# Prompt attention, first three query tiles: two pairs in flight on one PSUM bank per group, with constant products beside them

## What is computed

```python
s = jnp.einsum('bqgrd,bngd->bqgrn', qg, kc.astype(f32))
p = masked_softmax(s, (cmp_end[None, :] <= tq)[None, :, None, None, :])
o_cmp = jnp.einsum('bqgrn,bngd->bqgrd', p, vc.astype(f32))
...
o = g[..., 0:1] * o_cmp + g[..., 1:2] * o_slc + g[..., 2:3] * o_win
```

## Time and profile before

| | us |
|---|---|
| median of 3 runs | 3641.18 (3640.17 to 3641.56) |
| profiled execution, its own time | 3649.14 |
| span of its trace | 3647.7 |
| TensorE busy | 3419.4 |
| VectorE busy | 1495.8 |
| ScalarE busy | 868.0 |
| GpSimd busy | 642.9 |
| mean granted TensorE clock | 0.971 of full |
| prompt attention starts and ends in the span | about 939.5 and 1280 |

### The profile page before, as it was taken

The page is one execution under the profiler, slowest core; times in us unless marked ns, Lnnn a source line. Parts: engine busy times, 40 slices in busy tenths (PEclk is TensorE's granted clock), DMA queues, the critical chain, the costliest instruction groups (busy, mean ns, idle before and its releaser), DMA issues. The chain is left out here.

```text
span 3647.7 us, 64454 instructions
## 1 busy us (share of the span) xinstructions
PE 3419.4 (94%) x26955; PEld 2950.4 (81%) x26955; DVE 1495.8 (41%) x2726; ACT 868.0 (24%) x1649; POOL 642.9 (18%) x433
## 2 busy tenths in 40 slices
PE   8899998998878869999999998999999999999999
PEld 5666666554446649999999998888879999999999
DVE  4565666422466662323232323534424332322322
ACT  2333222011256622211011112433323211111110
POOL 0000000204000004222222223221113321222221
PEclk9999999999699989999999999999999999999999
DMA  2000000303200041211111102111113111111111
GB/s 105 22 20 8 26 10 12 135 24 82 77 1 2 1 167 41 76 58 52 45 41 46 48 33 102 35 54 66 38 76 118 53 50 36 51 35 45 47 40 66
DMA packets 77731, 186.33 MB, mean 51 GB/s; under 512 B 28412, under 2 KB 42556, under 8 KB 75468
## 3 DMA queue, kind: packets, MB, share of 16 engines
q1 hardware_dynamic: 60892, 141.85, 11.3%
q0 software_dynamic: 12272, 40.38, 3.4%
q10 hardware_dynamic: 4352, 1.05, 0.1%
HBM read 159.45 MB, written 27.92 MB: 51 GB/s over the span
## 5 line engine op out<-in xcount | busy, mean ns | idle before, releaser
L196 PE MATMUL ps<-ff_x,ff_wh 128*128 128x384 f32 (+1 forms) x3960 | 774.8, 328 | 0.0
L196 PEld LDWEIGHTS ps<-ff_x,ff_wh 128*128 128x128 f32 x3960 | 668.6, 188 | 0.8
L196 PE MATMUL ps<-ff_x,ff_wl 128*128 128x384 f32 (+1 forms) x2112 | 465.4, 328 | 0.0
L196 PEld LDWEIGHTS ps<-ff_x,ff_wl 128*128 128x128 f32 x2112 | 360.6, 188 | 0.0
L559 DVE TENSOR_TENSOR resid<-resid,ps 128x384 f32 (+1 forms) x240 | 113.3, 528 | 390.1 <-PE ps L196 390.1
L196 PE MATMUL ps<-ff_hh,ff_dh 128*128 128x384 f32 (+1 forms) x1056 | 233.8, 329 | 9.2 <-DVE ff_hl L551 4.8
L196 PE MATMUL ps<-ff_hh,ff_dl 128*128 128x384 f32 (+1 forms) x1056 | 233.4, 329 | 0.0
L196 PE MATMUL ps<-ff_hl,ff_dh 128*128 128x384 f32 (+1 forms) x1056 | 233.2, 329 | 0.0
L546 DVE TENSOR_TENSOR ff_prod<-ff_silu,ps 128x384 f32<-128x384 f32 x132 | 62.3, 528 | 349.5 <-PE ps L196 349.5
L279 POOL TENSOR_TENSOR ff_wl<-ff_w,ff_wh 128x1024 fp32r<-128x1024 f32 x44 | 111.9, 2543 | 500.4 <-ACT ff_wh L422 500.4
L196 PEld LDWEIGHTS ps<-ff_hh,ff_dh 128*128 128x128 f32 x1056 | 180.3, 188 | 11.0 <-DVE ff_hl L551 5.9
(11 more groups left out here) (609 smaller groups left out, 6192.2 us busy)
## 6 DMA issues: line engine op xcount, KB each, us to landing
ff_w<-in_wg SPq DMA_DIRECT2D x44, 512.0 KB, 3.2
ff_w<-in_wu SPq DMA_DIRECT2D x44, 512.0 KB, 3.3
ff_wd<-in_wd POOLq DMA_DIRECT2D x48, 256.0 KB, 3.0
ff_wd<-in_wd POOLq DMA_DIRECT2D x32, 320.0 KB, 3.3
rw_w<-in_w_rwkv SPq DMA_DIRECT2D x14, 512.0 KB, 3.4
ns_past<-in_cache_slc SPq DMA_DIRECT2D x48, 128.0 KB, 2.1
np_w<-in_w_nsa SPq DMA_DIRECT2D x8, 652.0 KB, 7.8
resid<-in_x SPq DMA_DIRECT2D x1, 4352.0 KB, 14.9
```

The costliest lines, as they stand in the source:

```text
L196: mm = pe.matmul(g.ps[:, bank + c, 0:n], w[:, k, :], x[:, o:o + n], start=(first and i == 0), stop=(last and i == 2))
```

## The change

For the first 24 pairs (`short = 24`, query tiles 0 to 2, where the scores and the 63 compressed columns fit in one bank):

- the scores of a pair take one bank per group, 0 or 1 for group 0 and 2 or 3 for group 1, by the parity of the pair; the compressed part stands at column 448 of the bank;
- the scores of y wait for the exponentials of y-2 in place of y-1;
- TensorE issues scores 0 and 1, then 16 products of 384 columns in BF16 from constants (identity and masks), and then for each pair its transposes, the scores of y+2, the values of y-1;
- for pairs below 16, each step of transposes has one such product ahead of it, into the bank that the step writes;
- ScalarE does the exponentials of pairs 0 and 1 first; then for each pair all moves of y and then the exponentials of y+2;
- VectorE does the maxima of pairs 0 and 1 and the scaling of pair 0, and then for each pair the scaling of y+1 ahead of the maxima of y+2.

From pair 24 on all is as before.

```diff
+    short = 24
+    def score_banks(y, gr):
+        b = 2 * gr + (y % 2 if y < short else 0)
+        return g.ps[:, b:b + 1, :] if y < short else g.ps[:, b:b + 2, :]
+    def compressed_of(y, gr):
+        at = 448 if y < short else 768
...
-                if y >= 1:
+                if y >= short:
                     pe.wait_ge(expd, 2 * y)
+                elif y >= 2:
+                    pe.wait_ge(expd, 2 * y - 2)
...
                 if x >= 2:
                     pe.wait_ge(moved, x - 1)
+                if y < 16:
+                    spare_products(pe, g.ps[:, 4 + x % 2, 0:3 * P], ident, every_mask, 1)
...
             scores(0)
+            scores(1)
+            spare_products(pe, g.ps[:, 4, 0:3 * P], ident, every_mask, 16)
             for y in range(len(pairs)):
-                if y + 1 < len(pairs):
+                if short <= y + 1 < len(pairs):
                     scores(y + 1)
                 xs = of_pair[y]
                 for x in xs[0:2]:
                     turn(x)
+                if y + 2 < short:
+                    scores(y + 2)
                 if y >= 1:
                     values(y - 1)
...
             act.wait_ge(blank, 2)
-            exponent(0, 0)
-            exponent(0, 1)
+            for y in range(2):
+                for gr in range(2):
+                    exponent(y, gr)
             for y in range(len(pairs)):
                 xs = of_pair[y]
+                if y < short:
+                    for x in xs:
+                        move(x)
+                    for gr in range(2):
+                        if y + 2 < short:
+                            exponent(y + 2, gr)
+                        if y == short - 1:
+                            exponent(short, gr)
+                    continue
...
-            maxima(0, 0)
-            maxima(0, 1)
+            for y in range(2):
+                for gr in range(2):
+                    maxima(y, gr)
+            for gr in range(2):
+                weights(0, gr)
             for y in range(len(pairs)):
-                for gr in range(2):
-                    weights(y, gr)
+                for z in ([y + 1] if y + 1 < short else [] if y < short else [y]):
+                    for gr in range(2):
+                        weights(z, gr)
                 if y % 8 == 1 and y > 8:
                     store(y // 8 - 1)
-                if y + 1 < len(pairs):
+                for z in ([y + 2] if y + 2 < short else [y + 1] if short <= y + 1 < len(pairs) else []):
                     for gr in range(2):
-                        maxima(y + 1, gr)
+                        maxima(z, gr)
```

More of the change, by code:

```diff
@@ L980, in size, with scores_of @@
         return len(keys(t, part)) + part
+    short = 24
+    def score_banks(y, gr):
+        b = 2 * gr + (y % 2 if y < short else 0)
+        return g.ps[:, b:b + 1, :] if y < short else g.ps[:, b:b + 2, :]
+    def scores_of(y, gr, n):
+        return score_banks(y, gr).rearrange("p a n -> p (a n)")[:, 0:n]
+    def compressed_of(y, gr):
+        at = 448 if y < short else 768
+        return score_banks(y, gr).rearrange("p a n -> p (a n)")[:, at:at + NCMP]
     steps = [(y, a, min(4, 2 * size(y) - a)) for y in range(len(pairs)) for a in range(0, 2 * size(y), 4)]
@@ L999, in nsa_prompt @@
         ident, causal, window = (masks[:, x, :] for x in range(3))
+        every_mask = masks[:, :, :].rearrange("p a n -> p (a n)")
         @block.sync
@@ L1041, in scores @@
                     for gr in range(2):
-                        mm = pe.matmul(g.ps[:, 2 * gr + a // 512, 0:m], q[gr], g.kT[f[gr], 1 + part, lo + a:lo + a + m], start=True, stop=not inside)
+                        mm = pe.matmul(scores_of(y, gr, n)[:, a:a + m], q[gr], g.kT[f[gr], 1 + part, lo + a:lo + a + m], start=True, stop=not inside)
                 for a in range(0, n, 512):
@@ L1046, in scores @@
                         for gr in range(2):
-                            mm = pe.matmul(g.ps[:, 2 * gr + a // 512, j * P - a:j * P - a + P], ident, over[j], start=False, stop=(j == inside[-1]))
+                            mm = pe.matmul(scores_of(y, gr, n)[:, j * P:j * P + P], ident, over[j], start=False, stop=(j == inside[-1]))
                 if part == 1:
-                    out = [g.ps[:, 2 * gr + 1, 256:256 + NCMP] for gr in range(2)]
+                    out = [compressed_of(y, gr) for gr in range(2)]
                     for gr in range(2):
@@ L1104, in exponent @@
                 n = len(keys(t, part)) * P
-                b = 2 * gr
                 act.wait_ge(maxed, i + 1)
@@ L1109, in exponent @@
                 x = prob[part][:, gr, :]
-                s = g.ps[:, b:b + 2, :].rearrange("p a n -> p (a n)")[:, 0:n]
-                a = act.activation(x[:, 0:n], s, ACT.Exp, bias=top[:, i % 4, 0:1], accum_out=total[:, i % 4, 0:1])
+                a = act.activation(x[:, 0:n], scores_of(y, gr, n), ACT.Exp, bias=top[:, i % 4, 0:1], accum_out=total[:, i % 4, 0:1])
                 if part == 1:
-                    a = act.activation(x[:, 640:640 + NCMP], g.ps[:, b + 1, 256:256 + NCMP], ACT.Exp, bias=top[:, i % 4, 1:2],
+                    a = act.activation(x[:, 640:640 + NCMP], compressed_of(y, gr), ACT.Exp, bias=top[:, i % 4, 1:2],
                                        accum_out=total[:, i % 4, 1:2])
@@ L1148, in maxima @@
                     dve.wait_ge(expd, i - 3)
-                s = g.ps[:, b:b + 2, :].rearrange("p a n -> p (a n)")[:, 0:n]
-                m = dve.tensor_reduce(top[:, i % 4, 0:1], s, AX, ALU.max, negate=True)
+                m = dve.tensor_reduce(top[:, i % 4, 0:1], scores_of(y, gr, n), AX, ALU.max, negate=True)
                 if part == 1:
-                    m = dve.tensor_reduce(top[:, i % 4, 1:2], g.ps[:, b + 1, 256:256 + NCMP], AX, ALU.max, negate=True)
+                    m = dve.tensor_reduce(top[:, i % 4, 1:2], compressed_of(y, gr), AX, ALU.max, negate=True)
                 m.then_inc(maxed, 1)
```

## The result

The changed kernel takes 3614.44 us (median of 4 runs, 3610.66 to 3618.15), the kernel before 3641.37 in the same comparison; the ratio is 0.9921, with a 95% interval of 0.9906 to 0.9936: 26.9 us less (23 to 34). The prediction said 3624.9 and 3615 to 3636, so it had the sign and was too small: the measured time lies 0.6 us under its range.

A forecast was written before the change was run, and what follows sets the result against it. It took a chain round the engines (scores, maximum, two exponentials), part at half clock, as the bound. First wait to 948.6 plus 80.0 us of laps and stores gave a 16.3 us gain: 3624.9 us, range 3615 to 3636.

The forecast's parts named there:

- The new ring: Lap of the first 24 pairs: transposes, their move, next pair's exponentials, scaling; two laps 6.33, 7.66, 7.81 us by tile.
- T(3): T(y) is the end of scaling of pair y; the forecast had T(2) = 948.6 and T(23) = 1028.6.
- first parts: Lap from a pair's last scaling to the next pair's first exponential, through transposes and moves: 1.01 to 1.71 us.
- the sum: Laps of pairs 3 to 23 plus stores, 80.0 us, added to T(2) = 948.6 to give T(23) = 1028.6.
- first wait: Start of the stage, bridged by sixteen products in 3.2 us; first transposes at about 945.4, T(2) = 948.6.
- second parts: Lap from first exponential to last scaling: 1.57 and 2.32 us in tile 0, 2.26 and 2.82 in tile 2.
- The stores: Two stores on VectorE in the first 24 pairs, each delaying a maximum, 1.9 us in all.
- Rival 4: More than forecast: the new ring isn't closed and TensorE's work bounds the three tiles; 3613 us, chance 0.05.
- Rival 1: Clock stays at half until tile 2, half clock stretching products by 1.76; gain 5.2 us, 3636.0, chance 0.12.
- Rival 2: Only the clock helps and overlap brings nothing in the first 24 pairs; gain 9 us, 3632, chance 0.08.
- Rival 3: Slower: the clock stays at half through tile 2 and beyond; 3654 us, chance 0.05.
- The 16.3 us: Forecast gain: scores of pair 24 start at 1027.65 against 1043.91, all of it reaching the end.

The follow-up runs named there:

- f3: The changed kernel without any of the constant products: 3617.46 us, and 74.81 us for the first 24 pairs.
- f2: The changed kernel with ScalarE moving the transposes of pair y+1 ahead of the exponentials of y+2: 3632.80 us, and 89.20 us for the first 24 pairs.
- i4: The changed kernel with scores of y+2 ahead of transposes of y and their maxima ahead of scaling of y+1: 3612.91 us, 67.11 us for the 24 pairs.
- i2: The changed kernel without the sixteen products, the one per step kept: 3620.86 us (one run), and 77.21 us for the first 24 pairs.
- f4: The kernel before with the constant products alone, one pair at a time: 3647.07 us, ratio 1.0006, and 105.42 us for the first 24 pairs.
- i3: The changed kernel with eight products in the first wait in place of sixteen: 3612.66 us (one run), and 71.02 us for the first 24 pairs.
- f1: The changed kernel again with no edit, timed in more rounds: 3614.73 us against 3645.48 for the kernel before, ratio 0.9919.
- j1: The changed kernel with scores and maxima of y+2 moved ahead and only the sixteen products: 3607.54 us, and 65.95 us for the first 24 pairs.
- i1: The changed kernel with the sixteen products only, none per step: 3607.42 us (one run), and 69.45 us for the first 24 pairs.

## Why the prediction was wrong

**What bounds the kernel before.** (The slow slice of the earlier trace rows, 912 to 1003 us, is the eleventh, not the twelfth.) Right: the ring scores, maximum, exponentials, closed by the wait for the exponentials. f3, which takes away that wait and holds no clock, gains 28.7 us of 32.7.

**The new ring.** This is the step that failed: "ScalarE moves the transposes of y+1 and only then takes the exponentials of y+2". The loop of the change reads, at pair y, moves of y and then exponentials of y+2. I had numbered the laps by the pair just scaled (y+1) and put its move in place of the one that the queue has there. The moves of y are done when pair y+1 is scaled (955.42 + 0.39 against T(3) = 956.46), so neither the moves nor the wait for transposes lies on the ring. The real ring is maximum of one group, exponentials, scaling; TensorE touches it only ahead of compressed pairs, by 0.2 to 0.5 us. The first parts that the trace shows are 0.23, 0.37 and 0.50 us ahead of plain pairs in tiles 0, 1 and 2, where the prediction has 1.43, 1.71 and 1.23, and 0.7, 0.7 to 1.0 and 0.6 to 1.0 ahead of compressed ones, where it has 1.01, 1.43 and 1.50. Two laps are 4.8, 5.4 to 5.9 and 6.0 to 6.4 us. From T(2) to T(23) the trace has 62.7 us (953.77 to 1016.45) where the sum has 80.0: 17.3 less. The first wait was 0.9 us longer than predicted, which leaves the 16.4 us by which the 24 pairs came out shorter than the sum (70.86 against 87.3). f2 has the queue as I read it and takes 80.3 us there: the prices were sound on the whole, the order wasn't. The second parts were within 0.2 us of the trace (1.57 and 2.32; 1.82 and 2.56; 2.06 and 2.80). The stores were priced too low: the two laps with a store take 7.0 and 7.75 us, 1.1 to 1.8 more each, where the sum had 1.9 for both.

**Rival 4** was this case, with a chance of 0.05: I asked whether the ring is closed as I think and answered from the same misread line. Its 3613 us is within 2 us of the result by luck: it is the middle between the forecast and TensorE's own work, and no row put it there. In tile 2 TensorE does bound, at 25.89 of 27.36 us, and opening the ring gains nothing there (27.47 in i4); in tiles 0 and 1 it doesn't, as i4 shows by gaining 1.3 and 2.5 us.

**First wait.** "Sixteen products then take 3.2 us" and the clock at 1.00 throughout were wrong: the clock fell at 946.8 after all, and the sixteen took 4.4 us, about 0.17 each at full and 0.32 at half clock. Transposes start 6.2 us into the stage, not 5.0. The price at full clock, 0.20, was near.

**Rival 1, the clock at half until tile 2,** didn't happen; f3 and i2 show that its prices were too high. In i2, at half clock and with the step's product, two laps of tile 0 take 6.8 us and not 7.6, and the clock was back 29 us into the stage, in the second pair of tile 1. It gains 26.3 us, f3 28.7, and not 5.2. **Rival 2, only the clock helps,** is refuted by f4 (-1.9 us) and f3. The Trainium skill (TensorE: Matmul & The Clock Gate, "HAM oscillation") has a kernel in which PSUM double buffering gave no further gain; f3, in which two banks per group and the new order of the queues give 28.7 us, came out otherwise; here TensorE had waited for the bank in lap after lap. The Trainium skill (same page, "A second HAM failure mode: psum-queue depth-cycling") describes a kernel whose clock oscillates while it cycles through PSUM banks. The changed kernel's two traces show 1.00 through tiles 1 and 2 and one fall of 3 to 4 us behind them; i3 had one more in tile 1, f2 two, in tiles 0 and 1. So there were single falls, and no oscillation from step to step. **Rival 3** had nothing for it.

**The base.** The 16.3 us were taken off 3641.18 us. Against the 21 runs of f1 the base was 4 us low, which hid part of the error: there the gain is 30.8 us and was missed by 14.5. The 24 pairs alone show 32.7 us, twice the 16.3.

## What to carry to other kernels

When a change reorders hand-written queues, write the new queue of each engine out for three consecutive pairs, with their numbers, before pricing a lap: here most prices held within 0.3 us a lap, and one index cost half the gain. Reading from a slot that is freed two pairs later takes out the wait, but what then bounds is the queue in which two engines call on each other in turn; put each step as early as its data allows, as j1 does. Products issued to hold the clock paid here only in the one long wait ahead of dense work (5.4 us, f3 against i1); they gave nothing where the waits go on (f4), and one per step cost 1.4 us or more. Price them apart from the overlap.

## What was unexpected in the hardware

Half clock cost less than the length of single products suggests. The same four score products take 1.76 times as long at half clock (rival 1), but two laps of tile 0 take 6.3 us in f3 (3.15 from scores to scores) where they take 4.7 in i1, at full clock: 1.34 times. In i1 TensorE was busy 16.89 of 18.83 us of tile 0 with the sixteen products in it, so that it had idle time to give. Products from constants brought the clock back in the first wait in each of the seven versions that have them there, and didn't keep it: it fell again twice in f4, twice in f2 and once in i3 within the 24 pairs. The same idle time at the same place of the program was followed by half clock in some runs and by full clock in others: 1.51 us in i3 and the changed kernel, and 1.75 us ahead of pair 27, where the step's product, long over by then, goes with the fall in thirteen traces of thirteen.
